# Second feed-forward block: transposing three of four groups by 32x32 blocks on VectorE and sixteen SBUF transfers instead of on TensorE

## The chip, the cores and the metric

One core of a Trainium2 chip runs the whole program. The metric is the device time of one execution in microseconds (us).

## The reference, cut to what matters

Two transformer-like blocks of width 2048 run one after the other over 256 rows. Each has a feed-forward part with 8192 inner columns; all weights are float32.

```python
# first block
m = rms_norm(h, pre_mlp_norm[i]) @ w_up[i]
m = jnp.square(jax.nn.relu(m)) @ w_down[i]
# second block
def sq_relu_mlp(h, w1, w2):
    return jnp.square(jax.nn.relu(h @ w1)) @ w2
```

The hidden rows `square(relu(x @ w1))` come out of the first product with tokens on the 128 partitions. The second product needs them with the inner columns on the partitions, so every hidden 128x128 square has to be transposed.

## The kernel before, in words

Every product of the kernel is cut into **chunks** of 512 output columns, and a chunk into **pieces** of 256 rows of weight (eight pieces for a depth of 2048). SyncE loads a piece (512 KB) into one of four slots of `raw`; ScalarE copies it rounded into `whi` (L706); VectorE subtracts, `wlo = raw - whi` (L1936); TensorE then makes twelve matmuls of 128x128 by 128x512: high by high, low by high, high by low (L1400). The loops run the same pieces in the same order on every engine and are tied by counting semaphores: SyncE loads piece p when VectorE has done piece p-4, ScalarE splits piece p+3 when TensorE has done piece p-1. A function `chunk(..., extra={u: f})` on an engine calls `f` just before it handles its u-th piece of that chunk; on ScalarE and VectorE that is the split of the piece three further on, on SyncE `f` comes after the load.

The feed-forward part `mlp` runs four blocks (`i`, NSB = 4) of 2048 inner columns. A block is eight chunks (`SEQ`): U0 to U3 make the hidden columns, D0 to D3 multiply them by the second weight matrix. After chunk U*c*:

- ScalarE evacuates PSUM with Relu into `rrow` (L903), GpSimd squares it into `sqrow` (L2681), each in two instructions of 128x512.
- In the next chunk TensorE makes eight 128x128 transposes of `sqrow` into two PSUM banks, ahead of its piece 3 (`turn_hidden`, L1610).
- At slot 4 of that chunk (`TURN_U`) ScalarE copies the two banks to `hhi` (L894) and VectorE makes `hlo` from them (L2208).

Those four inner groups of 512 columns feed D0 to D3. In the last block of the first feed-forward part and in the second block of the second one, SyncE also loads `w_mod` (L647) and VectorE multiplies it (L2142), at some of the slots. In chunk 17 of the second part, slot 6, ScalarE's queue writes a column of 2048 single numbers to DRAM (`gate_column_out`, L957).

Of the kernel before, what the change touches and what calls it, by code (L numbers as in the profile page):

```python
# [7 lines left out]
ALU = mybir.AluOpType  # L8
# [6 lines left out]
P = 128  # L15
# [5 lines left out]
HD = 128  # L21
# [102 lines left out]
def build(nc, I, out):  # L124

    ctx = ExitStack()
    with ctx:
# [143 lines left out]

        scratch = nc.dram_tensor("x_mid", (P, TH, D), F32, kind="Internal").ap()
# [36 lines left out]
        early_in = sem("early_in")  # L309
# [16 lines left out]
        gqk_in = sem("gqk_in")  # L326
# [25 lines left out]
        e_out = sem("e_out")  # L352
        e_in = sem("e_in")
        lb_out = sem("lb_out")
        lb_rows = sem("lb_rows")
# [201 lines left out]

        block = ctx.enter_context(nc.Block())
# [3 lines left out]
        def _(sp):  # L562
# [26 lines left out]
            def head_gains():  # L589
                for n, name in enumerate(("q_norm", "k_norm")):  # L590
                    sp.dma_start(g2[:, n], bass.AP(I[name].tensor, 0, [[0, P], [1, HD]])).then_inc(gqk_in, 16)

            def tables():
                sp.dma_start(early[:], I["k_early"]).then_inc(early_in, 16)
# [103 lines left out]
        def _(act):  # L698
# [75 lines left out]
            def spread_gains():  # L774
                act.wait_ge(gqk_in, 32)
# [108 lines left out]
            def mlp(k, u0, scale, extras):  # L884
                p0, g0 = plan[k]
                t0 = TG[k][0]
                for i in range(NSB):
                    for j, (kind, c) in enumerate(SEQ):
                        g = g0 + len(SEQ) * i + j

                        def turned(c=SEQ[j - 1][1], i=i):
                            for h in range(2):
                                act.wait_ge(t_done, i * 8 + (t0 + 2 * c + h + 1))
# [4 lines left out]
                        def relu(c=c, i=i, g=g):  # L898
                            act.wait_ge(sq_done, i * 8 + (2 * (u0 + c) + 2))
                            if scale and i == 0 and c == 0:  # L900
                                act.wait_ge(rstd_done, RMS["norm1"] + 1)
                            for th in range(TH):
# [5 lines left out]
                              extra=merge(extras.get(len(SEQ) * i + j, {}), {TURN_U: turned} if j and SEQ[j - 1][0] == "U" else {}))  # L908

            def embedding_out():  # L910
                act.wait_ge(acc_free, plan["mlp1"][1] + 2)
                act.dma_start(e_scratch, erow[:]).then_inc(e_out, 16)

            def context_in():
                act.wait_ge(e_out, 16)
# [49 lines left out]
            def embedding_in():  # L965
                act.wait_ge(t_done, TG["normc"][0] + 8)
                act.dma_start(erow[:], e_scratch).then_inc(e_in, 16)
# [145 lines left out]
            for c in range(14):  # L1113
# [7 lines left out]
                elif c < 12:  # L1121
                    if c == 10:
                        act.wait_ge(spill, 16)
# [190 lines left out]
            def row_squares(th):  # L1314
                act.wait_ge(reload, 16)
# [57 lines left out]
        def _(pe):  # L1373
# [224 lines left out]
            def mlp(k, u0, extras, first):  # L1598
                p0, g0 = plan[k]
                t0 = TG[k][0]  # L1600
                for i in range(NSB):
                    for j, (kind, c) in enumerate(SEQ):
                        def turn_hidden(c=SEQ[j - 1][1], i=i):
                            pe.wait_ge(sq_done, i * 8 + (2 * (u0 + c) + 4))
                            for h in range(2):
# [6 lines left out]
                                ins.then_inc(t_done, 1)  # L1612

                        def hidden(u, i=i):
                            return (lambda: pe.wait_ge(t_hi, i * 8 + (TG[k][1] + u + 1))), (lambda: pe.wait_ge(t_free, i * 8 + (t0 + u + 1)))
# [1145 lines left out]
```

## Time and profile before

| | us |
|---|---|
| median of three runs (2822.43 to 2824.7) | 2822.73 |
| the profiled execution's own time | 2820.31 |
| its span | 2818.7 |
| TensorE busy in the span | 2782.9 |
| VectorE busy | 1997.9 |
| ScalarE busy | 1374.9 |
| GpSimd busy | 146.9 |

The span is the time between the first and the last instruction; the execution's own time has some 1.6 us around it. TensorE's busy time is a sum over overlapping matmuls, so it says that the engine is nearly always occupied and not that it is at its peak. The granted TensorE clock over the span is 0.996 of the full 2.4 GHz.

### The profile page before, as it was taken

What the parts mean: (1) busy time and instruction counts of PE and PEld (TensorE: products, weight loads), DVE (VectorE), ACT (ScalarE), POOL (GpSimd) and SP (SyncE); (2) the same over time, 40 slices, a digit from 0 to 9 for tenths busy, and PEclk for the clock granted to TensorE, in tenths of its full rate; (3) what the DMA queues carried; (4) which work ended last, traced back from release to release, by engine and by line L of the source; (5) the groups of instructions that cost most, each with busy time, mean ns of one, the idle gap of its engine ahead of it and who ended that gap; (6) DMA issues with size and microseconds to landing.
All of it is one profiled execution on the core that took longest, in us unless ns stands there. A gap on an engine that the chain in (4) does not pass through costs nothing.

```text
span 2818.7 us, 34529 instructions
## 1 busy us (share of the span) xinstructions
PE 2782.9 (99%) x12939; PEld 2314.6 (82%) x12939; DVE 1997.9 (71%) x2268; ACT 1374.9 (49%) x1719; POOL 146.9 (5%) x109
## 2 busy tenths in 40 slices
PE   9999999999999999999999999999989999999998
PEld 7887888888888888788888888898878888888887
DVE  5666877899997676757785488687975467754455
ACT  5446454443443455557444445754554444344443
POOL 0000010010000100000000001000001000010010
PEclk9999999999999999999999999999999999999999
DMA  8963887888888777555666666408855588775654
GB/s 256 215 203 108 279 277 267 280 273 284 287 277 309 260 252 234 196 194 171 217 192 198 198 182 186 134 6 309 307 183 182 193 276 275 255 202 190 191 186 157
DMA packets 332780, 623.09 MB, mean 221 GB/s; under 512 B 37015, under 2 KB 38807, under 8 KB 330903
## 3 DMA queue, kind: packets, MB, share of 16 engines
q1 hardware_dynamic: 323543, 601.52, 66.8%
q10 hardware_dynamic: 9088, 19.56, 1.9%
q8 instruction: 95, 1.56, 0.2%
q14 instruction: 54, 0.44, 0.0%
HBM read 614.68 MB, written 7.27 MB: 221 GB/s over the span
## 4 chain that ended last, share of the span: by engine, by line
PE 93%; DVE 3%; DMA 2%; ACT 1%; issue 1%; SPq 0%; DVEq 0%; POOLq 0%; POOL 0%; ACTq 0%
PE ps L1400 86%; DMA raw<-w_in 1%; PE ps L1379 1%; PE ps L1610 1%; PE ps L1813 1%; PE ps L1793 1%; DMA raw<-w_o 1%; PE ps L1421 1%; DVE wlo L1936 1%; PE ps L1831 1%; PE ps L1532 0%; ACT whi L706 0%; PE ps L1512 0%; DVE macc L2142 0%; DVE cf L2291 0%
## 5 line engine op out<-in xcount | busy, mean ns | idle before, releaser
L1936 DVE TENSOR_TENSOR wlo<-raw,whi 128x1024 fp32r<-128x1024 f32 x940 | 1168.5, 1249 | 731.3 <-ACT whi L706 726.8
L706 ACT ACTIVATE whi<-raw 128x1024 fp32r<-128x1024 f32 x939 | 994.9, 1060 | 1222.6 <-PE ps L1400 1111.2
L1400 PE MATMUL ps<-whi,hhi 128*128 128x512 f32 x2032 | 549.5, 392 | 1.5 <-DVE yrow L2159 1.5
L1400 PE MATMUL ps<-whi,hlo 128*128 128x512 f32 x2032 | 544.0, 389 | 0.0
L1400 PE MATMUL ps<-wlo,hhi 128*128 128x512 f32 x2032 | 543.4, 389 | 0.2 <-DVE wlo L1936 0.2
L1400 PEld LDWEIGHTS ps<-wlo,hhi 128*128 128x128 f32 x2032 | 381.4, 188 | 80.1 <-DVE wlo L1936 0.6
L1400 PEld LDWEIGHTS ps<-whi,hlo 128*128 128x128 f32 x2032 | 381.1, 188 | 79.7
L1400 PE MATMUL ps<-whi,xhi 128*128 128x512 f32 x1632 | 442.7, 393 | 1.6 <-issue 1.6
L1400 PEld LDWEIGHTS ps<-whi,hhi 128*128 128x128 f32 x2032 | 378.3, 188 | 79.5 <-DVE yrow L2159 1.9
L1400 PE MATMUL ps<-whi,xlo 128*128 128x512 f32 x1632 | 440.1, 392 | 0.0
L1400 PE MATMUL ps<-wlo,xhi 128*128 128x512 f32 x1632 | 437.8, 390 | 0.0
L2142 DVE SCALAR_TENSOR_TENSOR macc<-mraw,cols,macc 128x512 f32<-128x512 f32 x504 | 367.1, 758 | 4.5
L1400 PEld LDWEIGHTS ps<-wlo,xhi 128*128 128x128 f32 x1632 | 307.5, 188 | 64.5
L1400 PEld LDWEIGHTS ps<-whi,xlo 128*128 128x128 f32 x1632 | 306.1, 188 | 63.5
L1400 PEld LDWEIGHTS ps<-whi,xhi 128*128 128x128 f32 x1632 | 304.4, 189 | 62.8 <-issue 1.9
L2681 POOL TENSOR_TENSOR sqrow<-rrow 128x512 f32<-128x512 f32 x64 | 93.1, 1475 | 1154.3 <-ACT rrow L903 1154.3
L2390 DVE SCALAR_TENSOR_TENSOR yT<-uT,cols,yT 128x252 f32<-128x252 f32 (+17 forms) x144 | 52.8, 428 | 0.0
L2661 POOL TENSOR_TENSOR stat<-stat 128x2 f32<-128x2 f32 x9 | 9.8, 1085 | 643.0 <-DVE stat L2148 442.4
L2208 DVE TENSOR_TENSOR hlo<-ps,hhi 128x512 fp32r<-128x512 f32 x64 | 41.0, 681 | 0.0
L1217 ACT ACTIVATE dec<-ps 128x1024 f32<-128x1024 f32 x32 | 32.5, 1023 | 17.1 <-PE ps L1793 10.5
L1813 PE MATMUL ps<-qD,kD 128*128 128x128 f32 x256 | 34.7, 279 | 3.6 <-DVE qD L2466 2.1
L1813 PEld LDWEIGHTS ps<-qD,kD 128*128 128x128 f32 x256 | 31.0, 191 | 5.1 <-DVE qD L2466 3.1
(312 smaller groups left out, 1476.6 us busy)
## 6 DMA issues: line engine op xcount, KB each, us to landing
raw<-w_in SPq DMA_DIRECT2D x296, 512.0 KB, 4.4
raw<-mlp_w SPq DMA_DIRECT2D x256, 512.0 KB, 3.8
mraw<-w_mod SPq DMA_DIRECT2D x384, 256.0 KB, 5.0
raw<-w_up SPq DMA_DIRECT2D x128, 512.0 KB, 4.6
raw<-w_down SPq DMA_DIRECT2D x128, 512.0 KB, 4.9
raw<-w_o SPq DMA_DIRECT2D x32, 512.0 KB, 5.3
raw<-w_ple_gate SPq DMA_DIRECT2D x32, 512.0 KB, 3.7
raw<-w_out SPq DMA_DIRECT2D x32, 512.0 KB, 5.9
```

The lines of the kernel that those rows point to most:

```text
L706: nc.scalar.activation(whi[:, s % NSLOT], raw[:, s % NSLOT], ACT.Copy).then_inc(hi_done, 1)
L1217: nc.scalar.activation(dst, src, ACT.Exp).then_inc(d_done, 1)
L1379: ins = nc.tensor.transpose(ps[:, TB[t % 2], c:c + P], src, ident)
L1400: ins = nc.tensor.matmul(ps[:, bank(par) + th], a[:, kt, th * P:(th + 1) * P], b[:, (s + u) % NSLOT, k], start=(kt == 0 and m == 0), stop= ...
L1421: ins = nc.tensor.matmul(ps[:, bank(g) + th], a[:, kt, th * P:(th + 1) * P], b[:, u % NSLOT, k], start=kt == 0 and m == 0, stop=kt == KT - ...
L1610: ins = nc.tensor.transpose(ps[:, TB[(t0 + h) % 2], a * T + th * P:a * T + (th + 1) * P], sqrow[:, th, f:f + P], ident)
L1813: ins = nc.tensor.matmul(o[:, (2 * hh + n) * P:(2 * hh + n + 1) * P], k[:, hh, n * P:(n + 1) * P], q[:, hh, t * P:(t + 1) * P], start=True ...
L1936: nc.vector.tensor_tensor(wlo[:, s % NSLOT], raw[:, s % NSLOT], whi[:, s % NSLOT].bitcast(F32), ALU.subtract)\
L2142: ins = nc.vector.scalar_tensor_tensor(out=a, in0=w, scalar=x, in1=a, op0=ALU.mult, op1=ALU.add)
L2208: nc.vector.tensor_tensor(hlo[:, kt:kt + 2], ps[:, TB[(t0 + h) % 2]].rearrange("p (a b) -> p a b", a=2), hhi[:, kt:kt + 2].bitcast(F32), A ...
L2390: nc.vector.scalar_tensor_tensor(out=y, in0=tap_part(uT[:, ct], ct, dd, True), scalar=wcol(TAPS // 2 + dd, ct), in1=y, op0=ALU.mult, op1=A ...
L2681: nc.gpsimd.tensor_tensor(sqrow[:, th], rrow[:, th], rrow[:, th], ALU.mult).then_inc(sq_done, 1)
```

## The change

For groups 0 to 2 of every block of the second feed-forward part, and of the last block of the first part, TensorE no longer transposes: 15 of the 32 groups. In their place, in the chunk after U*c*: at slot 2 VectorE makes two transposes of 32x32 blocks, `sqrow` to `hturned`; SyncE moves the blocks to their partitions by sixteen transfers of 32 partitions by 1 KB from `hturned` to `hgather`, queued behind its load of piece 1 of the chunk after next; at slot 7 ScalarE copies `hgather` to `hhi` and VectorE subtracts to `hlo`. `hturned` lies where `rrow` lies and `hgather` where `sqrow` lies, so the next Relu waits for the sixteen transfers and the next squares for `hlo`. Group 3 stays on TensorE. GpSimd's two loops over the blocks are written out, and some semaphores are merged (the head gains and the tables; the spills and the reloads).

```diff
+        BLK = P // STACK
+        hturned = at("hturned", [P, STACK, TH, STACK, BLK], F32, work_at + 32 * K)
+        hgather = at("hgather", [P, STACK, TH, STACK, BLK], F32, work_at + 36 * K)
...
+        def by_blocks(k, i, c):
+            return c < 3 and (k == "mlp2" or i == NSB - 1)
...
+            def blocks_moved(k, i, c):
+                n = VIA.index((k, i, c))
+                sp.wait_ge(ht_done, n + 1)
+                for g in range(STACK):
+                    for b in range(STACK):
+                        sp.dma_start(hgather[BLK * g:BLK * (g + 1), b], hturned[BLK * b:BLK * (b + 1), g]).then_inc(ht_in, 16)
...
+                        if 2 <= j <= 4 and by_blocks(k, i, j - 2):
+                            extra = merge(extra, {1: lambda i=i, j=j: blocks_moved(k, i, j - 2)})
...
             def spread_gains():
-                act.wait_ge(gqk_in, 32)
+                act.wait_ge(tables_in, 48)
...
+                        def blocks_high(c=j - 1, i=i):
+                            n = VIA.index((k, i, c))
+                            act.wait_ge(ht_in, 16 * STACK * STACK * (n + 1))
+                            for th in range(TH):
+                                nc.scalar.activation(hhi[:, 4 * c:4 * c + 4, th * P:(th + 1) * P].rearrange("p k (i b) -> p k i b", b=BLK),
+                                                     hgather[:, :, th].rearrange("p i k b -> p k i b"), ACT.Copy).then_inc(t_hi, 1)
...
                         def relu(c=c, i=i, g=g):
...
+                            if 1 <= c and by_blocks(k, i, c - 1):
+                                act.wait_ge(ht_in, 16 * STACK * STACK * (VIA.index((k, i, c - 1)) + 1))
...
-                              inserts=merge(extras.get(n, {}), {3: turn_hidden} if j and SEQ[j - 1][0] == "U" else {}, sum_inserts(k, n)),
+                              inserts=merge(extras.get(n, {}), {3: turn_hidden} if 1 <= j <= 4 and not by_blocks(k, i, j - 1) else {}, sum_inserts(k, n)),
...
+                        def blocks_turned(c=j - 1, i=i):
+                            dve.wait_ge(sq_done, i * 8 + 2 * (u0 + c) + 4)
+                            for th in range(TH):
+                                ins = nc.vector.transpose(hturned[:, :, th], sqrow[:, th].rearrange("p (k g b) -> p g k b", k=STACK, g=STACK))
+                            ins.then_inc(ht_done, 1)
+
+                        def blocks_low(c=j - 1, i=i):
+                            for th in range(TH):
+                                dve.wait_ge(t_hi, i * 8 + (h0 + 2 * c + th + 1))
+                                cs = slice(th * P, (th + 1) * P)
+                                nc.vector.tensor_tensor(hlo[:, 4 * c:4 * c + 4, cs].rearrange("p k (i b) -> p k i b", b=BLK),
+                                                        hgather[:, :, th].rearrange("p i k b -> p k i b"),
+                                                        hhi[:, 4 * c:4 * c + 4, cs].rearrange("p k (i b) -> p k i b", b=BLK).bitcast(F32),
+                                                        ALU.subtract).then_inc(t_free, 1)
...
+                                          {} if j < 1 or j > 4 else {2: blocks_turned, 7: blocks_low} if by_blocks(k, i, j - 1) else {TURN_U: turned}))
...
-                            pool.wait_ge(t_done, i * 8 + (TG[k][0] + 2 * c))
+                            if c and by_blocks(k, i, c - 1):
+                                pool.wait_ge(t_free, TG[k][0] + 8 * i + 2 * c)
```

## Rows read from the trace of the kernel before

**Rows 1.** The page: span, busy time by engine, chain of waits by engine.
```profile
span 2818.7 us, 34529 instructions
...
PE 2782.9 (99%) x12939; PEld 2314.6 (82%) x12939; DVE 1997.9 (71%) x2268; ACT 1374.9 (49%) x1719; POOL 146.9 (5%) x109
...
PE 93%; DVE 3%; DMA 2%; ACT 1%; issue 1%; SPq 0%; DVEq 0%; POOLq 0%; POOL 0%; ACTq 0%
```

**Rows 2.** Waits of TensorE, 2080 to 2800 us: total, times, longest.
```profile
PE ps L1379 <- ACT xs L1342: 6.5, 1, 6.5
PE ps L1400 <- issue: 1.6, 1, 1.6
```

**Rows 3.** Timeline of TensorE in chunk 17: start, duration, line, operation, [idle before].
```profile
2476.46 1.07 PE L1400 MATMUL ps<-whi,xhi 128*128 128x512 f32 x4
...
2479.18 1.07 PE L1400 MATMUL ps<-whi,xhi 128*128 128x512 f32 x4
...
2484.62 1.04 PE L1610 MATMUL ps<-small,sqrow 128*128 128x128 f32 x8
...
2499.12 1.07 PE L1400 MATMUL ps<-whi,xhi 128*128 128x512 f32 x4
```

**Rows 4.** Timeline of GpSimd, the squares of chunk 16.
```profile
2477.90 3.02 POOL L2681 TENSOR_TENSOR sqrow<-rrow 128x512 f32<-128x512 f32 x2 [107.15 <-ACT rrow L903]
```

**Rows 5.** Timeline of VectorE in chunk 17: splits of its pieces 4 and 5.
```profile
2480.88 1.21 DVE L1936 TENSOR_TENSOR wlo<-raw,whi 128x1024 fp32r<-128x1024 f32 x1
2483.25 1.23 DVE L1936 TENSOR_TENSOR wlo<-raw,whi 128x1024 fp32r<-128x1024 f32 x1 [1.16 <-ACT whi L706]
```

**Rows 6.** Timeline of VectorE in the block with w_mod: the products at slot 2.
```profile
2303.75 1.53 DVE L2142 SCALAR_TENSOR_TENSOR macc<-mraw,cols,macc 128x512 f32<-128x512 f32 x2
```

**Rows 7.** VectorE's groups by shape, whole span: busy us, mean ns | idle before.
```profile
L2208 DVE TENSOR_TENSOR hlo<-ps,hhi 128x512 fp32r<-128x512 f32 x64 | 41.0, 681 | 0.0
...
L2291 DVE RECIPROCAL rows<-rows 128x512 f32<-128x512 f32 x4 | 13.4, 3346 | 0.0
...
L2139 DVE TENSOR_SCALAR macc<-mraw,cols 128x512 f32<-128x512 f32 x8 | 3.7, 479 | 0.0
```

**Rows 8.** SyncE's issues by line: ns min/median/max, first and last start in us.
```profile
L600 SPq DMA_DIRECT2D raw<-mlp_w x256: 367/368/1099, 2068.9 to 2791.0; - x128
...
L617 SPq DMA_DIRECT2D bm<-bias_rows x32: 573/616/3060, 84.8 to 129.2; - x32
```

**Rows 9.** Timeline of SyncE near the start: small loads issued one behind another.
```profile
12.21 0.42 SPq L583 DMA_DIRECT2D vecs<-pre_ple_norm  x1
12.67 0.42 SPq L583 DMA_DIRECT2D vecs<-norm_pre_mix  x1
```

**Rows 10.** Landing time of the weight loads (L600) issued from 2440 to 2480 us.
```profile
DMA to landing us min/median/max: 3.5/4.0/4.6
```

**Rows 11.** DMA issues by line: size and median us to landing.
```profile
out<-res SPq DMA_DIRECT2D x8, 256.0 KB, 2.5
...
row_columns<-mcol ACTq DMA_DIRECT2D x1, 8.0 KB, 13.3
```

**Rows 12.** Timeline of ScalarE in chunks 17 and 18.
```profile
2476.66 1.09 ACT L903 ACTIVATE rrow<-ps 128x512 f32<-128x512 f32 x2 [1.60 <-PE ps L1400]
...
2479.43 1.06 ACT L706 ACTIVATE whi<-raw 128x1024 fp32r<-128x1024 f32 x1 [0.75 <-PE ps L1400]
...
2491.25 0.38 ACTq L957 DMA_DIRECT2D row_columns<-mcol  x1
...
2506.98 1.06 ACT L706 ACTIVATE whi<-raw 128x1024 fp32r<-128x1024 f32 x1 [5.63 <-DMA raw<-mlp_w]
```

**Rows 13.** A stretch of 5 us: busy of each engine, TensorE clock, DMA share, GB/s.
```profile
2496.00:2501.00 5.00, 5.00 (x24) 4.14 (x23) 1.49 (x2) 2.74 (x4) 0.43 (x1) 1.00 0.87 37
```

**Rows 14.** Lines of the merged semaphore: the tables' load, the copy that waits.
```profile
L594 SPq DMA_DIRECT2D early<-k_early x1: 468/468/468, 62.0 to 62.0; - x1
...
L777 ACT ACTIVATE gqk<-g x2: 398/720/1043, 82.0 to 83.0; 128x1024 f32<-128x1024 f32 x1, 128x256 f32<-128x256 f32 x1
```

More of the change, by code:

```diff
@@ L556, in build, with skipped, hidden_turned @@
             tc = [tc[0] + groups, tc[1] + groups * counted]
+        def by_blocks(k, i, c):
+            return c < 3 and (k == "mlp2" or i == NSB - 1)
+        VIA = [(k, i, c) for k in ("mlp1", "mlp2") for i in range(NSB) for c in range(4) if by_blocks(k, i, c)]
+        def skipped(k, i, c):
+            return 2 * sum(by_blocks(k, i, b) for b in range(c))
+        def hidden_turned(k, i, c, h):
+            return TG[k][0] + 8 * i + 2 * c + h + 1 - (skipped(k, i, c) if c < 3 else 0)
         block = ctx.enter_context(nc.Block())
@@ L907, in mlp @@
                         chunk(p0 + 8 * (len(SEQ) * i + j), evac,
-                              extra=merge(extras.get(len(SEQ) * i + j, {}), {TURN_U: turned} if j and SEQ[j - 1][0] == "U" else {}))
+                              extra=merge(extras.get(len(SEQ) * i + j, {}), {} if j < 1 or j > 4 else
+                                          {7: blocks_high} if by_blocks(k, i, j - 1) else {TURN_U: turned}))
             def embedding_out():
                 act.wait_ge(acc_free, plan["mlp1"][1] + 2)
-                act.dma_start(e_scratch, erow[:]).then_inc(e_out, 16)
+                act.dma_start(e_scratch, erow[:]).then_inc(spill, 16)
             def context_in():
-                act.wait_ge(e_out, 16)
+                act.wait_ge(spill, 16)
                 act.dma_start(trow[:], rows_of(I["ctx_2"][0])).then_inc(ctx_in, 16)
@@ L2217, in mlp @@
                               extra=merge(extras.get(n, {}), mod_totals(k, n), mod_extra(k, n, mod_product),
-                                          {TURN_U: turned} if j and SEQ[j - 1][0] == "U" else {}))
+                                          {} if j < 1 or j > 4 else {2: blocks_turned, 7: blocks_low} if by_blocks(k, i, j - 1) else {TURN_U: turned}))
             NM, NP, NX = 5 * KT, 4 * KT, 2 * KT
@@ L2273, in _ @@
             d_first = c_first + 32
-            mlp("mlp1", place({0: lambda: post0_res(3), 1: low1(3), 2: low1(4), 3: low1(5), 4: low1(6), 5: low1(7), 6: norm1_mean_square,
+            mlp("mlp1", 0, place({0: lambda: post0_res(3), 1: low1(3), 2: low1(4), 3: low1(5), 4: low1(6), 5: low1(7), 6: norm1_mean_square,
                                c_first + 5: mod_of_mixer, c_first + 6: mixer_gains,
@@ L2618, in _ @@
             last = 8 * (len(SEQ) * NSB - 4)
-            mlp("mlp2", place({0: lambda: [low4(0), norm4_row(2)], 1: lambda: [low4(1), norm4_row(3)],
+            mlp("mlp2", 16, place({0: lambda: [low4(0), norm4_row(2)], 1: lambda: [low4(1), norm4_row(3)],
                                **{g: (lambda g=g: low4(g)) for g in range(2, 8)}, 137: last_mods, **{last + 8 * c + 13: (lambda c=c: post4_gain(c)) for c in range(3)}}))
@@ L2678, in mlp @@
                             pool.wait_ge(acc_free, i * len(SEQ) + (g0 + j + 2))
-                            pool.wait_ge(t_done, i * 8 + (TG[k][0] + 2 * c))
+                            if c and by_blocks(k, i, c - 1):
+                                pool.wait_ge(t_free, TG[k][0] + 8 * i + 2 * c)
+                            elif c:
+                                pool.wait_ge(t_done, hidden_turned(k, i, c - 1, 1))
+                            else:
+                                pool.wait_ge(t_done, TG[k][0] + 8 * i)
                             nc.gpsimd.tensor_tensor(sqrow[:, th], rrow[:, th], rrow[:, th], ALU.mult).then_inc(sq_done, 1)
-            with pool.Fori(0, NSB) as i:
+            for i in range(NSB):
                 mlp(i, "mlp1")
@@ L2731, in _ @@
             nc.gpsimd.tensor_tensor(stat[:, 10:12], stat[:, 4:6], stat[:, 64:66], ALU.pow).then_inc(rstd_done, 1)
-            with pool.Fori(0, NSB) as i:
+            for i in range(NSB):
                 mlp(i, "mlp2")
```

34 lines of the change are left out of this document (17 added, 17 removed).

## The prediction, made before the changed kernel ran

> **What bounds the kernel now.** I read the page first: TensorE is busy 99% of the span and holds 93% of the chain that ended last [rows 1]. The waits of TensorE over the second feed-forward part come next: two waits, 8.1 us in all, at its very beginning [rows 2]; from there to the end it waits for nobody. So time falls here only by taking work from TensorE, and rises only if something is late enough to make it wait. The third view is its timeline in chunk 17, the one that transposes group 0 of block 2 [rows 3]. A piece of twelve matmuls takes 2479.18 - 2476.46 = 2.72 us. Between pieces 2 and 3 stand eight transposes, and the whole chunk lasts 2499.12 - 2476.46 = 22.66 us, against 8 x 2.72 = 21.76 us without them: a group costs 0.90 us of the bound engine.
>
> **TensorE's part.** 15 groups go: 15 x 0.90 = 13.5 us, all on the path. Group 3 of each block stays, as do the 17 groups outside the condition.
>
> **VectorE's part.** Two block transposes of 128x512 come in at slot 2. The trace has no such instruction; its 128x512 operations lie between 0.48 us and 3.35 us, and most of them at 0.68 us [rows 7]. I take 0.68 us, as the subtraction that it stands beside, and keep 1.0 to 6.7 us for the two. In chunk 17 the squares end at 2477.90 + 3.02 = 2480.9 [rows 4], and VectorE is free from 2480.88 + 1.21 = 2482.1 [rows 5]: it doesn't wait for them. The two end at 2483.5, the split of piece 5 behind them at 2484.7 instead of 2484.5. At the upper end that split would end at 2490.0; TensorE needs it 1.8 us (two thirds of a piece) into piece 5, at 2476.46 + 13.6 + 1.8 = 2491.9, so even that is covered by the three pieces that the splits are ahead. Where w_mod is multiplied (6 of the 15 groups) 1.53 us of products stand ahead at slot 2 [rows 6] and the split comes about 1.4 us later than before. `hlo` costs two instructions of the same size as before [rows 7]; the copies to `hhi` likewise. They only move from slot 4 to slot 7, and TensorE wants group 2, the last of them, four pieces later in D0.
>
> **SyncE's part.** This is where the change can lose. Sixteen issues stand in the in-order queue between the loads of piece 1 and piece 2 of the chunk after next. Load 1 follows the split of piece 5, which VectorE does after its transposes, so SyncE's new wait adds nothing. No issue between SBUF addresses is in the trace. Bounds: 0.37 us, a weight load [rows 8], and 3.06 us, the longest bias load, among 32 whose median is 0.62 us [rows 8]. I take 0.46 us, the step from one small load to the next [rows 9], as the nearest in size: 16 x 0.46 = 7.4 us. In chunk 17: load 1 at 2484.7, transfers from 2485.1 to 2492.5, then load 2, some 5 us later than now; it lands 4.0 us later [rows 10], at 2496.5, and its split by ScalarE (1.06 us) ends at 2497.6. TensorE comes to that piece ten pieces after the chunk's start, at 2476.46 + 27.2 = 2503.7. Cover left: 6.1 us. With 0.62 us it is 3.6 us; the cover is gone at 0.46 + 6.1 / 16 = 0.84 us a transfer, and the gain of the group at 0.90 us. In the groups with w_mod, 1.4 us later, 4.7 us are left (at 0.62 us 2.1 us). Both upper bounds together, 0.62 us and 6.7 us of transposes, make these six groups 3.2 us late each and the other nine 1.7 us.
>
> That a late load alone does no harm is seen in the trace: at 2506.98 ScalarE had waited 5.63 us for a load [rows 12], and TensorE had no wait there [rows 2].
>
> **The transfers' landing.** The last is issued at 2492.0; the fastest kind in the trace lands in 2.5 us, the slowest in 13.3 [rows 11]. I take 2.5, the plain transfer: 2494.5. ScalarE comes to slot 7 six pieces and one split in, 2476.46 + 16.3 + 1.3 = 2494.1, waits 0.4 us, copies for 1.2 us and is ready for load 2 at 2495.7, before that has landed. Behind the wait stand that split, the next Relu (2498.2, unmoved) and with it the next squares. To make TensorE late the landing must come after 2503.7 - 1.06 - 1.2 = 2501.4, that is take 9.4 us.
>
> The Trainium skill speaks against this part: "DMA: Bandwidth & Descriptors", section "Anatomy of one DMA", puts a fixed cost of about 2.0 us on every transfer, and its "Rules for kernel authors" say that below 64 KB one pays mostly overhead and should join small transfers. These are 32 KB each. The same section says that most of the fixed cost is the wait for the last byte's receipt, and small loads issued 0.46 us apart [rows 9] agree that the queue doesn't hold the next issue for it; what it does if the transfers follow one another is rival 4, priced from rows there.
>
> **One place without cover.** In chunk 17, slot 6, ScalarE's queue starts the column write; it lands 13.3 us later [rows 11], and meanwhile the DMA engines move 37 GB/s at 87% busy [rows 13]. Now the loads of pieces 2 and 3 of chunk 18 have landed by then, or almost; with the change they are issued after 2492.5, into it. The write starts 0.9 us earlier, at about 2490.4, and holds until 2503.7. I estimate load 2 at 2504.5, split at 2505.6, against 2503.7: TensorE waits 2 us, once (0 to 4). It also stands behind about five of the transfers, which keeps the 4.
>
> **Edits at nothing.** The merged semaphores: the copy of head gains now also waits for the tables, whose load starts at 62.0, 20 us before that copy [rows 14]; the spills and reloads keep their order. GpSimd's loops written out: it is busy 5% of the span [rows 1]. If any of these covers failed, TensorE would wait at one place, once.
>
> **The sum.** 2820.31 (the profiled execution: 2818.7 of span and 1.6 around it) - 13.5 + 2.0 = 2808.8. The runs' median is 2.4 us above that execution, so on the median 2822.73 - 11.5 = 2811.2.
>
> **Rivals.**
> 1. Full cover, the column write included: 2822.73 - 13.5 = 2809.2. For it: the 5.63 us wait without effect [rows 12]. Against: no loads were held back then.
> 2. Partial cover. The six groups with w_mod, or the ones after a slow issue, lose 1 to 2 us each. Six at 1.5 us give 2811.2 + 9 = 2820; with the least loss, 0.5 us, 2814. It takes issues above 0.62 us or transposes near 3.35 us. For it: the bias loads' 0.62 us [rows 8]; against: these have more and shorter rows.
> 3. Slower: SyncE's queue becomes the bound. From 0.90 us a transfer each group loses more than it gains. At 1.2 us the sixteen take 19.2 us, 11.8 us more than my sum; less 6.1 us of cover (4.7 in six groups) TensorE waits 5.7 us nine times and 7.1 us six times, 94 us: 2811.2 + 94 = 2905. For it: single bias loads up to 3.06 us [rows 8]. Against: their median, and weight loads at 0.37 us.
> 4. Slower too, by another mechanism: the transfers don't overlap. Each 2.5 us behind the other [rows 11], the last lands 40 us after 2485.1, at 2525; ScalarE, stopped at slot 7, has the split ready at 2527.4, 23.7 us late, 15 times: 2811.2 + 356 = 3167. It decides from (2501.4 - 2485.1) / 16 = 1.0 us a transfer. It is the rule on small transfers taken at its word.
> 5. The change doesn't do what it says: TensorE is not the bound in these chunks and the time stays at 2822.7. Rows 2 and 3 speak against it; nothing for it.
>
> **How the numbers follow.** Chances: forecast 0.60, full cover 0.17, partial 0.11, SyncE's queue 0.07, transfers in a row 0.04, no effect 0.01. The range reaches from 2807.5, 1.7 us below full cover for the spread of a median (the three runs spread 2.3 us), to 2820, the dear end of partial cover; past it lie rivals 3 to 5 and the rest of 2, some 0.14. A difference under 0.2% (5.6 us, so above 2817.1) can't be told from none here. Forecast, full cover and half of partial are faster, 0.82; the other half and no effect are the same, 0.07; rivals 3 and 4 are slower, 0.11.
>
> **What would show it.** Right: chunks that lose the transposes last 21.76 us; no transposes but group 3's; sixteen issues in about 7.4 us, the next load some 5 us late; ScalarE's waits moved to the transfers and loads at slot 7 without a wait of TensorE, save one near the column write. Wrong: waits of TensorE for `whi` or `wlo` at piece 2 of a chunk (SyncE's queue), issues above 0.84 us, a landing above 9 us, or transposes so long that the splits fall behind.

## The result and the profile after

The changed kernel is slower. Its median is 2834.39 us (six runs, 2832.74 to 2836.83) against 2822.58 us of the kernel before on the same chip: a ratio of 1.0046, 95% interval 1.0036 to 1.0056, 11.8 us. Forecast were 2811.2 us in a range of 2807.5 to 2820. The profiled execution took 2835.27 us.

The page answers to [rows 1]: TensorE is busy 4.9 us less (forecast were 13.5; behind some waits its matmuls take longer, as shown further down), the span is 14.8 us longer, and ten points of the chain that ended last have gone from TensorE to VectorE, to SyncE's transfers (L674) and to DMA. In the first line of the last pair stand shares by engine, in the second by line.

```profile
span 2833.5 us, 34492 instructions
...
PE 2778.0 (98%) x12819; PEld 2304.9 (81%) x12819; DVE 2022.2 (71%) x2298; ACT 1377.7 (49%) x1719; POOL 143.8 (5%) x109
...
PE 83%; DVE 5%; SPq 4%; DMA 3%; issue 2%; ACT 2%; POOL 0%; DVEq 0%; POOLq 0%; ACTq 0%
PE ps L1434 76%; SPq L674 4%; DVE wlo L1971 2%; DMA raw<-mlp_w 1%; PE ps L1413 1%; PE ps L1848 1%; ACT whi L730 1%; PE ps L1828 1%; DVE macc L2177 1%; DMA raw<-w_o 1%; DMA hgather<-hturned 1%; PE ps L1455 1%; PE ps L1644 1%; PE ps L1866 1%; DVE hturned L2242 0%
```

The waits of TensorE in the second part after the change (in total, times, longest) answer to [rows 2]. The two old ones stand; 13.2 us are new, for ScalarE's split and for GpSimd's squares (ahead of group 3's transposes, L1644).

```profile
PE ps L1434 <- ACT whi L730: 10.0, 7, 3.1
PE ps L1413 <- ACT xs L1376: 6.6, 1, 6.6
PE ps L1644 <- POOL sqrow L2736: 3.2, 3, 1.1
PE ps L1434 <- issue: 1.6, 1, 1.6
```

The new instructions after the change (ns min/median/max; then the landing) answer to [rows 7, 8 and 11]: the block transposes are as forecast, 0.68 us; the landing too, 2.1 us for 2.5; an issue takes 0.59 us for 0.46, and 0.04 us lie between two.

```profile
L674 SPq DMA_DIRECT2D hgather<-hturned x240: 507/591/1482, 925.6 to 2735.2; - x120
...
L2242 DVE STREAM_TRANSPOSE hturned<-sqrow x30: 661/684/707, 922.7 to 2723.6; 128x512 f32<-128x512 f32 x30
...
  ACT hhi L919: 72.8, 15
...
DMA to landing us min/median/max: 1.8/2.1/10.5
```

The indented line is the point: ScalarE, which was to wait 0.4 us a group, waited 72.8 us in 15 groups. What comes before that wait is seen in the chain of waits after the change, here for the third group of block 0 (start, duration, what; of the sixteen transfers the first and the last are shown):

```profile
2169.02 4.07 DMA raw<-mlp_w
...
2173.11 0.04 ACT whi L730
...
2176.12 3.26 DVE wlo L1971 x2
2179.39 1.22 DVE hturned L2242 x2
2180.60 1.12 DVE wlo L1971
...
2181.74 0.37 SPq L615
...
2182.15 0.51 SPq L674
...
2191.83 0.59 SPq L674
...
2192.47 1.84 DMA hgather<-hturned
```

What follows is in the timeline of ScalarE after the change (start, duration; in brackets the idle time before and what ended it):

```profile
2194.33 1.16 ACT L919 ACTIVATE hhi<-hgather 128x512 fp32r<-128x512 f32 x2 [6.04 <-DMA hgather<-hturned]
2197.11 1.06 ACT L730 ACTIVATE whi<-raw 128x1024 fp32r<-128x1024 f32 x1 [1.62 <-DMA raw<-mlp_w]
2198.08 1.07 ACT L936 ACTIVATE rrow<-ps 128x512 f32<-128x512 f32 x2
```

From the block transposes to the copy to `hhi` it is 14.9 us. But the copy is not the last wait: ScalarE then stands 1.62 us more for a weight load, the one that SyncE issues behind the sixteen transfers, and only then come the split, the Relu and the squares. So it is in 12 of the 15 groups, by 1.5 to 2.0 us; in the other three this load lands just as the copies end. The timeline of GpSimd after the change shows the squares of one chunk and of the next.

```profile
2175.22 3.09 POOL L2736 TENSOR_TENSOR sqrow<-rrow 128x512 f32<-128x512 f32 x2 [20.10 <-ACT rrow L936]
2199.22 3.09 POOL L2736 TENSOR_TENSOR sqrow<-rrow 128x512 f32<-128x512 f32 x2 [20.91 <-ACT rrow L936]
```

They are 24.00 us apart, where a chunk without transposes lasts 21.76 us. The split behind the late load is as far from the one before it (2197.11 - 2173.11 = 24.00), and the chain says why. In its first lines the load behind the sixteen transfers of the group before lands (at 2173.09); its split, the Relu and the next split follow on ScalarE, then VectorE's splits (until 2179.38), behind them the block transposes, then the load of piece 1, the sixteen issues, and the next load behind them. That is a closed round, longer than a chunk; each group of a block starts later than the one before it, against TensorE. A second round runs beside it, over the landing of the sixteen and ScalarE's stop at slot 7. Without the 1.62 us for the load the 24.00 would be some 22.4 us (an estimate): that round too is longer than a chunk, but the shorter of the two.

To find where the time went, I subtracted the start of the n-th split of VectorE in the trace of before from that in each other trace (940 splits in both). Change of that difference by stage, in us, negative where time is won; three whole groups are worth 2.7 us. One profile scatters by some 2 us in stages where nothing is changed (third column).

```
kernel                   first part,  stage   unchanged  second part, block
                         last block   behind  stages     0     1 (w_mod)  2 (column)  3
after                      +1.1       +4.8     0.0      -0.9     +5.8       +4.7     -1.2
e1 one transfer            -2.7       +2.9    +1.6      -2.7     -2.7       -2.7     -2.7
e2 four batches            +8.1       +4.5    +2.5      +2.3    +16.6      +13.0     +3.3
e3 without w_mod            0.0       +0.2    +0.4      -1.5      0.0       +4.9     -1.1
e4 GpSimd's queue          -2.0       +3.1    +1.8      -2.7     +4.8       +4.2     -2.7
e5 through DRAM            -2.7       +2.4    +1.6      -2.7     +0.2       +3.9     -2.7
e9 queue alone             +1.8       -1.3    -0.7       0.0     +3.7       +3.2      0.0
e10 one late               +2.1       +3.0    -0.3      -2.7     +7.0       +5.2     -2.7
e11 loop open               0.0       +0.2    +2.0      +1.4    +10.0       +7.5     +1.7
e12 loop open, GpSimd       0.0       -0.7    +2.3      -2.7     -2.7       -2.7     -2.7
e13 loop open, half         0.0       -1.6    +0.1      -2.7     -2.7       -2.7     -2.7
e14 half each              -2.7       +4.1    +0.1      -2.7     -2.7       -2.7     -2.7
```

So most of the loss of the changed kernel lies in the two blocks with `w_mod`, in the block with the column write, and in the stage behind the first part; the two plain blocks (0 and 3) win 0.9 and 1.2 us where each should win 2.7.

### The profile page after: what moved, and what is told of

It is laid out like the page before. It is cut to its first block, busy times and chain, and to the rows that moved or that the text cites. A ratio compares the mean times of both kernels' runs of the same rounds, so it can differ in the third digit from the quotient of the medians.

```text
span 2833.5 us, 34492 instructions
## 1 busy us (share of the span) xinstructions
PE 2778.0 (98%) x12819; PEld 2304.9 (81%) x12819; DVE 2022.2 (71%) x2298; ACT 1377.7 (49%) x1719; POOL 143.8 (5%) x109
## 4 chain that ended last, share of the span: by engine, by line
PE 83%; DVE 5%; SPq 4%; DMA 3%; issue 2%; ACT 2%; POOL 0%; DVEq 0%; POOLq 0%; ACTq 0%
PE ps L1434 76%; SPq L674 4%; DVE wlo L1971 2%; DMA raw<-mlp_w 1%; PE ps L1413 1%; PE ps L1848 1%; ACT whi L730 1%; PE ps L1828 1%; DVE macc L2177 1%; DMA raw<-w_o 1%; DMA hgather<-hturned 1%; PE ps L1455 1%; PE ps L1644 1%; PE ps L1866 1%; DVE hturned L2242 0%
## 5 line engine op out<-in xcount | busy, mean ns | idle before, releaser
L2177 DVE SCALAR_TENSOR_TENSOR macc<-mraw,cols,macc 128x512 f32<-128x512 f32 x504 | 373.7, 773 | 4.6
L2249 DVE TENSOR_TENSOR hlo<-hgather,hhi 128x512 fp32r<-128x512 f32 x30 | 19.4, 689 | 63.9 <-ACT hhi L919 63.9
L919 ACT ACTIVATE hhi<-hgather 128x512 fp32r<-128x512 f32 x30 | 17.3, 626 | 72.8 <-DMA hgather<-hturned 72.8
L1251 ACT ACTIVATE dec<-ps 128x1024 f32<-128x1024 f32 x32 | 32.6, 1025 | 17.1 <-PE ps L1828 10.5
```

What stands on the lines that cost most here:

```text
L1251: nc.scalar.activation(dst, src, ACT.Exp).then_inc(d_done, 1)
L2177: ins = nc.vector.scalar_tensor_tensor(out=a, in0=w, scalar=x, in1=a, op0=ALU.mult, op1=ALU.add)
```

## The experiments

The kernel before had medians of 2819.53 us (beside e0 to e3), 2819.51 (e4, e5, e9, e10), 2819.86 (e11, e12) and 2821.16 (e13, e14); a difference is always against the one run beside it.

**e0, the edits alone.** No group goes by blocks; what is left are the merged semaphores and the written-out loops.

```diff
-            return c < 3 and (k == "mlp2" or i == NSB - 1)
+            return False
```

> All groups are transposed on TensorE again; only the written-out GpSimd loops and the merged semaphores of the change stay. Theory 1 (the loss is SyncE's sixteen issues, 0.63 us each in the changed kernel's trace, 10.1 us a group in front of the next weight loads): 2822.6, within 3 us. Rival (the other edits cost something: the changed kernel stands 1.3 us back after its first pieces and loses another 4.4 us near 1143 us, where no group is touched): about 2828.

Measured: 2819.64 us, ratio 1.0000 (0.9991 to 1.0009). The edits cost nothing.

**e1, one transfer.** One plain transfer of all 512 KB at the same place; the blocks are not moved to their partitions, so the hidden values are others.

```diff
-                for g in range(STACK):
-                    for b in range(STACK):
-                        sp.dma_start(hgather[BLK * g:BLK * (g + 1), b], hturned[BLK * b:BLK * (b + 1), g]).then_inc(ht_in, 16)
+                sp.dma_start(hgather[:], hturned[:]).then_inc(ht_in, 16)
```

> The sixteen transfers are one transfer of all 128 partitions and the same 512 KB, so the blocks don't reach their partitions and the hidden values of 15 groups are wrong. Theory 1 (issue time on SyncE): the waits of TensorE in the feed-forward parts vanish, 2834.4 less some 22 us, 2810 to 2816. Rival (the bytes between SBUF addresses take the DMA engines from the weights): no change, about 2834. Rival (the wait for the landing in front of ScalarE's splits): one transfer lands some 7 us earlier, so this too gives about 2812; the next run tells these two apart.

Measured: 2809.41 us, ratio 0.9964 (0.9950 to 0.9977), 10.1 us less. The timeline of ScalarE in e1 at the place of the chain above:

```profile
2182.65 1.14 ACT L917 ACTIVATE hhi<-hgather 128x512 fp32r<-128x512 f32 x2
...
2187.07 1.09 ACT L934 ACTIVATE rrow<-ps 128x512 f32<-128x512 f32 x2 [1.60 <-PE ps L1432]
```

And that of GpSimd in e1:

```profile
2166.47 3.02 POOL L2734 TENSOR_TENSOR sqrow<-rrow 128x512 f32<-128x512 f32 x2 [18.74 <-ACT rrow L934]
2188.23 3.02 POOL L2734 TENSOR_TENSOR sqrow<-rrow 128x512 f32<-128x512 f32 x2 [18.74 <-ACT rrow L934]
```

ScalarE doesn't stop, the Relu waits for TensorE as it should, and the squares are 21.76 us apart. Every block gains its 2.7 us, also the one with the column write. Neither the bytes nor VectorE's work nor the longer way through `hgather` costs anything: the sixteen issues do, or what waits for them.

**e2, four batches of four transfers**, behind the loads of pieces 1 to 4, so that no load waits for more than four issues.

```diff
-                            extra = merge(extra, {1: lambda i=i, j=j: blocks_moved(k, i, j - 2)})
+                            extra = merge(extra, {1 + g: lambda i=i, j=j, g=g: blocks_moved(k, i, j - 2, g) for g in range(STACK)})
```

> The sixteen transfers are issued four at a time, behind the loads of pieces 1, 2, 3 and 4. Theory 1: no load is held back by more than 2.5 us, so TensorE doesn't wait in groups without the column write; 2811 to 2816. Rival (ScalarE stops at slot 7 for the landing and is late with its splits): the last transfer is issued some 2 to 3 us later than in one burst, so more waits, 2836 to 2850.

Measured: 2865.98 us, ratio 1.0160 (1.0146 to 1.0174). That is slower than either expectation. Spreading the issues didn't help: the last transfer lands later still, and ScalarE stops for longer. ScalarE's wait in e2, from 2080 us to the end:

```profile
ACT hhi L918 <- DMA hgather<-hturned: 106.7, 12, 13.4
```

**e3, without the blocks that have w_mod**: nine groups.

```diff
-            return c < 3 and (k == "mlp2" or i == NSB - 1)
+            return c < 3 and k == "mlp2" and i != 1
```

> Only the nine groups of the second part's blocks 0, 2 and 3 by blocks; the six groups beside w_mod loads are transposed on TensorE. By the trace of the changed kernel the six lose 12.3 us and gain 5.4, the nine lose 10.4 and gain 8.1. Theory 1 (SyncE's queue has less room where it loads w_mod too): 2834.4 less 7, about 2827.5, and less than that if the 5.8 us outside the groups goes as well. Rival (each group costs the same 0.8 us net wherever it stands): 2822.6 + 9 x 0.8 = 2830.

Measured: 2824.27 us, ratio 1.0013 (1.0004 to 1.0023), 4.7 us more than before. Without the blocks with `w_mod` and without groups ahead of the stage behind the first part more than half of the loss is gone, but the column write's block still loses 4.9 us, and the plain ones win 1.1 to 1.5 instead of 2.7.

**e4, the same sixteen on GpSimd's queue.** No weight load stands behind them.

```diff
-                        sp.dma_start(hgather[BLK * g:BLK * (g + 1), b], hturned[BLK * b:BLK * (b + 1), g]).then_inc(ht_in, 16)
...
+                                    pool.dma_start(hgather[BLK * g:BLK * (g + 1), b], hturned[BLK * b:BLK * (b + 1), g]).then_inc(ht_in, 16)
```

> The same sixteen transfers, issued from GpSimd's queue behind the squares, not from SyncE's. Theory 1 as it stands after the first runs (a closed loop: VectorE's transposes, 10.1 us of issues, the landing, ScalarE stopped at slot 7, the next Relu, squares, the next transposes; it takes 23.2 to 26 us a round in the changed kernel against 21.76 us of a chunk): it depends on GpSimd's issue time, which no trace here shows; at 0.5 us or less the sixteen land before ScalarE comes to slot 7 and the time is 2808 to 2811; at 1 us or more the loop is longer than on SyncE, 2840 or above, though no weight load is held back. Rival (the loss is the weight loads held back in SyncE's queue): 2808 to 2812 at any issue time.

Measured: 2828.15 us, ratio 1.0036 (1.0023 to 1.0050). The issues in e4 (ns; who waited; landing):

```profile
L2732 POOL DMA_DIRECT2D hgather<-hturned x240: 496/496/697, 922.5 to 2720.4; - x120
...
  ACT hhi L910: 65.8, 15
...
DMA to landing us min/median/max: 2.4/4.7/13.5
```

Both expectations missed: the issues take 0.50 us, but the transfers land in 4.7 us (median) instead of 2.1. With no load held back ScalarE stops for nearly as long, and the blocks with `w_mod` and the column write lose nearly as much. The plain ones gain in full; so what they lose in the changed kernel goes with the held-back load.

**e5, through DRAM**: one transfer out and four back, five issues.

```diff
+                sp.dma_start(h_blocks, hturned[:].rearrange("p g t k b -> p g (t k b)")).then_inc(ht_out, 16)
...
+                    sp.dma_start(hgather[BLK * g:BLK * (g + 1)].rearrange("p i t k b -> p i (t k b)"), src).then_inc(ht_in, 16)
```

> The gather goes through a DRAM buffer: one transfer of 512 KB out behind load 1, four transfers of 128 KB back behind load 2; five issues, some 3 us of SyncE. Loop theory: out lands some 4 us after its issue, the last of the four back some 5 us later, at about the time that ScalarE comes to slot 7: waits of 0 to 2 us there, 2809 to 2816. Rival (held-back loads): load 3 waits 2 to 4 us at most, 2810. Rival (bytes on the DMA engines): another 15 MB of DRAM traffic in 15 groups, and slower than the changed kernel, 2834 or more.

Measured: 2820.70 us, ratio 1.0005 (0.9996 to 1.0014). The plain blocks gain in full, the one with `w_mod` loses what it gains, the one with the column write more. There are five issues instead of sixteen, but two landings in a row, and the time is above the 2809 to 2816 expected.

**e9, the queue alone.** TensorE transposes all groups as before; SyncE issues sixteen transfers of the same shape at the 15 places, from a table to an unused buffer, and no engine waits for them in the groups.

```diff
-                        sp.dma_start(hgather[BLK * g:BLK * (g + 1), b], hturned[BLK * b:BLK * (b + 1), g]).then_inc(ht_in, 16)
+                        sp.dma_start(spare[BLK * g:BLK * (g + 1), b], small[BLK * b:BLK * (b + 1)]).then_inc(ht_in, 16)
```

> TensorE transposes all groups as in the kernel before; SyncE also issues sixteen transfers of the same shape at the 15 places, from a constant table to a spare buffer, and nothing waits for them but the next sixteen. Loop theory: the held-back loads alone cost TensorE nothing in the nine groups without w_mod and up to 2 us in each of the six with it; 2819.5 to 2826. Rival (held-back loads are the loss): the changed kernel's loss without its gain, 2819.5 + 12 + 13.5 = 2845.

Measured: 2828.52 us, ratio 1.0033 (1.0021 to 1.0045): 9.0 us, between the two expectations. The queue costs something by itself: nothing in plain blocks, 3.7 and 3.2 us where `w_mod` or the column write comes on top, by loads that land late. A round has more room here than in the changed kernel, for a chunk with transposes lasts 22.66 us. ScalarE's wait in e9, from 2080 us to the end:

```profile
ACT whi L735 <- DMA raw<-mlp_w: 91.3, 39, 10.1
```

**e10, one late transfer**: e1's single transfer, issued behind the load of piece 4.

```diff
-                            extra = merge(extra, {1: lambda i=i, j=j: blocks_moved(k, i, j - 2)})
+                            extra = merge(extra, {4: lambda i=i, j=j: blocks_moved(k, i, j - 2)})
```

> One transfer of all 128 partitions, as in the run with one transfer (the hidden values of 15 groups are wrong), but issued behind load 4 and not load 1. SyncE is busy with it for 0.4 us. It lands about as late after the transposes as the sixteen, some 15 us. Loop theory: ScalarE waits 3 us at slot 7 and the rounds take some 24 us; 2825 to 2840. Rival (held-back loads): as with one early transfer, 2809.4.

Measured: 2831.55 us, ratio 1.0047 (1.0034 to 1.0061). The issue in e10, who waited, the landing:

```profile
L672 SPq DMA_DIRECT2D hgather<-hturned x15: 478/510/634, 931.6 to 2727.1; - x15
...
  ACT hhi L917: 95.6, 15
...
DMA to landing us min/median/max: 5.3/6.7/12.6
```

One issue of half a microsecond, put late, loses as much as sixteen put early; put early (e1) it loses nothing. So a late last landing is enough by itself, without a load held back; here too the plain blocks gain in full and the loss is in the others.

**e11, the round opened** (the 12 groups of the second part). `hturned` and `hgather` get room of their own, no Relu waits for the transfers, and `hhi` and `hlo` are made at slot 0 of the chunk after next; the sixteen stay on SyncE.

```diff
-                            if 1 <= c and by_blocks(k, i, c - 1):
-                                act.wait_ge(ht_in, 16 * STACK * STACK * (VIA.index((k, i, c - 1)) + 1))
...
-                                          {7: blocks_high} if by_blocks(k, i, j - 1) else {TURN_U: turned}))
+                              extra=merge(extras.get(len(SEQ) * i + j, {}), {0: blocks_high} if 2 <= j <= 4 and by_blocks(k, i, j - 2) else {},
```

> Block groups in the second part alone (12 groups, worth 12 x 0.9 = 10.9 us of TensorE). hturned and hgather get room of their own, so that no Relu waits for a transfer, and ScalarE and VectorE take the gathered values at slot 0 of the chunk after next, some 6 us later than slot 7. The sixteen transfers stay on SyncE. Theory (a loop from the block transposes over sixteen issues and the last landing to ScalarE's stop at slot 7, its next Relu, the squares and the next transposes is longer than a chunk): the loop is cut, the chunks last 21.76 us, TensorE waits for ScalarE's split at most in the groups with w_mod and at the column write, where weight loads are held back; time 2819.5 - 10.9 = 2808.6 plus 0 to 7 us of held loads: 2809 to 2816. Rival (the sixteen issues in SyncE's queue are the whole loss, by the weight loads behind them): cutting the loop changes nothing, the loss by group stays as in the changed kernel, 2826 or more.

Measured: 2840.98 us, ratio 1.0071 (1.0058 to 1.0085). My theory missed by 25 us, and the rival's 2826 or more came true: with the stop at slot 7 gone, the loss is larger. From 2080 us on ScalarE has no wait for `hgather` left, but one for weights, and the chain of waits of e11 shows the round through the weight loads alone. First the wait:

```profile
ACT whi L731 <- DMA raw<-mlp_w: 164.0, 58, 10.8
```

The chain (start, duration, what; the sixteen transfers left out):

```profile
2153.04 1.22 DVE hturned L2243 x2
2154.25 1.12 DVE wlo L1970
...
2155.39 0.37 SPq L615
...
2165.92 3.94 DMA raw<-mlp_w
...
2172.47 2.45 DVE hlo L2250 x2
...
2175.02 2.35 DVE wlo L1970 x2
2177.36 1.21 DVE hturned L2243 x2
```

The sixteen take SyncE to 2165.9; the next load lands at 2169.9; ScalarE and VectorE do their work on it, with `hlo` now among it; the next block transposes stand behind: 2177.36 - 2153.04 = 24.3 us. The sixteen are the longest stretch in this round. In the changed kernel the same round takes 23.2 to 24.0 us in the blocks without `w_mod`.

**e12, the same with the transfers on GpSimd's queue.**

```diff
-                        sp.dma_start(hgather[BLK * g:BLK * (g + 1), b], hturned[BLK * b:BLK * (b + 1), g]).then_inc(ht_in, 16)
...
+                            pool.wait_ge(t_free, TG[k][0] + 8 * i + 2 * c)
...
+                                    pool.dma_start(hgather[BLK * g:BLK * (g + 1), b], hturned[BLK * b:BLK * (b + 1), g]).then_inc(ht_in, 16)
```

> The same with the sixteen transfers issued on GpSimd's queue, so that no weight load stands behind them. Theory (loop and held loads, each with its part): both are gone; 2808.6 to 2811, no wait of TensorE in the second part but the two at its start. Rival (the loop alone is the loss, the queue costs nothing): the same time as with the transfers on SyncE, within 1 us. Third (sixteen small transfers load the DMA engines and delay the weights whoever issues them): waits of TensorE for the split stay, 2815 or more.

Measured: 2809.66 us, ratio 0.9963 (0.9949 to 0.9977), 10.2 us less than before where 12 x 0.9 = 10.8 were to be had, within the 2808.6 to 2811 expected. TensorE's waits from 2080 us on in e12 are the two of [rows 2] and no other:

```profile
PE ps L1402 <- ACT xs L1365: 6.5, 1, 6.5
PE ps L1423 <- issue: 1.6, 1, 1.6
```

**e14, eight transfers on each queue**: the changed kernel with its 15 groups, its slot 7 and its shared buffers.

```diff
-                for g in range(STACK):
+                for g in range(2):
...
+                            for g in range(2, STACK):
+                                for b in range(STACK):
+                                    pool.dma_start(hgather[BLK * g:BLK * (g + 1), b], hturned[BLK * b:BLK * (b + 1), g]).then_inc(ht_in2, 16)
```

> The changed kernel with all its 15 groups and its slot 7, but eight of the sixteen transfers on SyncE's queue and eight on GpSimd's. Theory (two loops longer than a chunk, one through the last landing and ScalarE's slot 7, one through the weight loads behind the sixteen issues): eight issues take 5.1 us instead of 10.1, the last landing comes 10.3 us after the block transposes start instead of 14.7, before ScalarE gets to slot 7 (12.2 us with one transfer), and the next loads are held 5 us instead of 10. Both loops are then shorter than 21.76 us and nothing adds up: the full 13.5 us, less about 3 given back at the first part's end and 0 to 3 at the column write: 2809 to 2813. Rival (each issue costs in proportion, wherever the sum stands): half of the 25 us that the changed kernel loses on its full gain comes back, 2821 to 2823.

Measured: 2813.94 us, ratio 0.9972 (0.9962 to 0.9981), 7.2 us less than before. (The expectation's 2809 to 2813 was worked out from a kernel before of 2819.5; this one had 2821.16.) ScalarE's waits for the transfers from 2080 to 2800 us are 8.3 us in e14 (below) instead of 60.0 in the changed kernel, and TensorE waits nowhere but at the two places of [rows 2]; each block of the second part gains its 2.7 us.

```profile
ACT hhi L921 <- DMA hgather<-hturned: 8.3, 3, 6.2
```

**e13, the opened round with eight on each queue** (12 groups; the same split of the transfers in e11).

> The opened loop (12 groups, gathered values taken at slot 0 of the chunk after next), eight transfers on SyncE and eight on GpSimd. Theory: the loop through the weight loads, 24.3 us with sixteen issues on SyncE (block transposes, issues, landing of the next load, copies and splits), falls by 5.1 us to 19.2, under a chunk's 21.76: no waits of TensorE for the split, 2808.6 to 2811. Rival (in proportion): half of the 31 us between the two versions of the opened loop, about 2825.

Measured: 2812.98 us, ratio 0.9970 (0.9958 to 0.9981), 8.2 us less than before; that is above the 2808.6 to 2811 expected, which again started from 2819.5. Its profile gains 2.7 us in every block. Halving the issues on SyncE took away not half of e11's loss but all of it. The loss is that of a round against a chunk, with a threshold, not a price for each issue.

## Why the prediction was wrong, by its own steps

**TensorE's part** held: a group is worth 0.9 us wherever nothing holds TensorE up (e1, e12 to e14: 2.7 us for three groups). One thing was overlooked. The statement that TensorE waits for nobody was read from the second part alone [rows 2]; behind the first part's last block there is a stage with a wait of its own. Here are the waits of TensorE from 880 to 1200 us after the change.

```profile
PE ps L1413 <- DVE hlo L1989: 4.6, 1, 4.6
PE ps L1434 <- ACT whi L730: 2.4, 2, 1.7
PE ps L1644 <- POOL sqrow L2736: 1.2, 1, 1.2
```

The first is 2.3 us long in the kernel before. In e1, which gains 2.7 us ahead of it, TensorE comes earlier and waits 4.6 us there, so that the gain of these three groups is given back; in e14 too. In the changed kernel, which comes to the stage with a loss, the wait is 4.6 us as well, so an earlier TensorE is not its whole cause. The kernels with no block groups ahead of this stage (e3, e11, e12, e13) lose nothing there (0.2 us at the most). 12 x 0.9, not 15, were to be had.

**VectorE's part and the edits at nothing** held: 0.684 us a transpose, e0 at ratio 1.0000. (That most of VectorE's 128x512 operations take 0.68 us was misread: the most frequent, the product with `w_mod`, takes 0.76 us. Nothing hung on it.)

**SyncE's part** was mis-sized: 16 x 0.635 us (0.59 and the gap of 0.04) = 10.2 us and not 7.4. By the prediction's own account that was no harm: at 0.62 us it left 3.6 us of cover (3.5 by its numbers), 2.1 with `w_mod`. But this cover was worked out for one group that finds all splits three pieces ahead. A held-back load that lands late leaves the next group with less, and the account doesn't carry that over. e9, where only the queue is left, loses 0.0 in the plain blocks and 3.7 with `w_mod`.

**The transfers' landing is the step that failed**, at the words "the next Relu (2498.2, unmoved) and with it the next squares". The prediction held its two late comers, the last transfer and the load behind the sixteen, against the moment when TensorE needs the split (2503.7, 6.1 us of cover). But the Relu stands behind that split in ScalarE's queue, and for it the prediction's own numbers leave 0.6 us: the load lands at 2496.5, its split ends at 2497.6, the Relu is due at 2498.2. The 2.8 us that the issues took longer are enough to move it.

Measured, ScalarE waited twice in a group. For the transfers it was 2.42 us in the first group of block 0 (forecast 0.4; the longer issues, less 0.4 us of quicker landing, make 2.8), then 3.72 and 6.04 us. After the copies it waited 1.57, 1.71 and 1.62 us more for the load, so that the load, and not the landing, set the Relu. Splits, squares and block transposes are behind the Relu, issues behind the transposes: the delay comes round. From one group of a block to the next, the landings of that load are 23.2 to 24.0 us apart in blocks 0, 2 and 3 of the second part and 24.5 to 26.5 us in the two blocks with `w_mod`. I priced the wait once for each group and asked whether TensorE would feel it ("take 9.4 us"); I should have added up the round and compared it with 21.76 us.

Both rounds go through the sixteen issues, and either one alone costs time: the one over the landing in e10 (one issue, late: slower by 12.0 us) and e4 (no load behind the sixteen: slower by 8.6 us), in both without a loss in the plain blocks; the queue and its held-back loads in e9 (slower by 9.0 us) and e11 (21.1 us). With both short (e1, e12, e13, e14) the second part's gain is there in full. So it is shown that the loss comes from rounds through the sixteen issues that are longer than a chunk; how the loss in the blocks with `w_mod` and the column write divides between the two rounds is not separated.

**With w_mod** the products at slot 2 lengthen either round; the forecast's rival 2 (partial cover) had the place and the condition, an issue above 0.62 us (0.635 with the gap), but 1.5 us for each group where block 1 lost 5.8 + 2.7 = 8.5 us, 2.8 a group.

**The column write** was priced by the weight loads that it delays, 2 us; e9 measures 3.2 us for that. Not foreseen was that seven of the sixteen small transfers, those issued after the write began at 2501.79 us, fall into it as well. The timeline of ScalarE in the changed kernel there:

```profile
2515.14 1.15 ACT L919 ACTIVATE hhi<-hgather 128x512 fp32r<-128x512 f32 x2 [9.60 <-DMA hgather<-hturned]
2517.27 1.07 ACT L936 ACTIVATE rrow<-ps 128x512 f32<-128x512 f32 x2
```

The longest landing is 10.5 us, above the 9.4 us that the prediction named as its limit; the block gained nothing and lost 4.7 us.

**TensorE's clock** added to it. After the wait of 3.15 us that ends at 2381 us and that of 2.15 us that ends at 2517 us the mean granted clock of the next 9 us is 0.81 in the changed kernel; before the waits it was 1.00. The clock is 1.2 GHz for part of the stretch, and 9 x (1 - 0.81) = 1.7 us of full speed are lost each time, which the sum of the waits doesn't hold. Against its full gain of 10.8 us the second part lost 19.2 us (10.8 and the 8.4 by which its four blocks are longer); 13.2 us are new waits, 3.4 us these two stretches, and the rest was not traced. The first two lines are from the timeline of TensorE (four matmuls take 1.07 us elsewhere), the others are sums over a stretch. Columns: span, busy time and count of PE, PEld, DVE, ACT and POOL, granted clock, DMA share, GB/s.

```profile
2381.49 2.04 PE L1434 MATMUL ps<-whi,hhi 128*128 128x512 f32 x4 [3.15 <-ACT whi L730]
2517.42 1.65 PE L1434 MATMUL ps<-whi,xhi 128*128 128x512 f32 x4 [2.15 <-ACT whi L730]
...
2372.00:2381.00 9.00, 6.34 (x28) 4.90 (x27) 2.52 (x3) 2.23 (x4) 0.00 (x0) 1.00 0.51 140
2381.00:2390.00 9.00, 8.51 (x35) 7.01 (x36) 8.49 (x8) 4.88 (x7) 2.55 (x2) 0.81 1.02 378
...
2518.00:2527.00 9.00, 9.00 (x34) 7.30 (x33) 7.55 (x8) 5.65 (x6) 2.10 (x2) 0.81 0.80 264
```

**The rivals.** SyncE's queue as the bound (2905 us) was refuted by its own price, 0.635 us against 0.90, and still the load held behind the queue was what the round waited for last. Transfers in a row (3167 us) didn't happen: they land 2.1 us after their issue, sixteen of them within 12 us. The Trainium skill, "DMA: Bandwidth & Descriptors", "Rules for kernel authors", wants small transfers joined. In e1 that wins, for another reason than the landing: its one transfer of 512 KB lands in 6.3 us (its median), where the chain of the changed kernel has 12.2 us from the first issue to the last landing (2194.31 - 2182.15), most of it issues. It is not the only way: e12 has the full gain in the second part with sixteen small ones. The fixed cost of about 2.0 us, which the prediction put on every transfer, stands in the section "Anatomy of one DMA" of that page of the Trainium skill for transfers issued from GpSimd. The landings from SyncE come near it, 1.8 us at the least and 2.1 us in the median; those from GpSimd in e4 are longer, 2.4 and 4.7 us.

**What stays open.** Why the stage behind the first part gives the gain back even when TensorE comes to it earlier: in e1 ScalarE does three splits of `w_in` there 2 to 3 us earlier than in the kernel before, but the fourth, behind a load, at 1119.42 us against 1117.81. A column of single numbers is written in that stage too; whether it delays the load was not tried. In e3 the plain blocks lose 1.2 to 1.6 us of their 2.7; in eight of its nine groups the held-back load again came last, but no run took it alone out of e3.

## What to carry to other kernels

When work goes from the bound engine to a way over several queues, write down every round that closes from one iteration to the next (who waits for whom, until the same instruction comes again), add up its steps, and compare the sum with the time of one iteration of the bound engine: below it the whole gain is there, above it the excess is paid each time, and cover worked out for one iteration says nothing. Hold each late comer against the first thing that stands behind it in its queue (here the Relu), not only against the bound engine. A wait put into an in-order queue delays all that stands behind it, so look at what those instructions release. Where a round is too long, shorten its longest stretch (here: half of the issues on another queue) before restructuring.

## What the runs showed of the hardware

- An issue of a transfer of 32 partitions x 1 KB between SBUF addresses holds SyncE's queue for 0.59 us, longer than that of a weight load of 512 KB (0.37 us, [rows 8]); GpSimd's queue issues the same in 0.50 us, SyncE one of 512 KB between SBUF addresses in 0.51 us (e1).
- The same transfer lands in 2.1 us (median) in the changed kernel, where SyncE issues no load between the sixteen, and in 4.7 us when GpSimd issues it and SyncE's loads run beside it (e4). The queue alone is not shown to be the reason: in e14, with eight on each queue, it is 4.1 us from SyncE and 4.2 us from GpSimd.
- While a column of 2048 single numbers is written to DRAM (12.3 us to landing in the changed kernel), transfers between SBUF addresses are slow as well: 9.24 us for the last of the sixteen in the chain of the changed kernel, against 1.84 us in block 0.
- A wait of TensorE of 2.15 us was followed by a granted clock of 0.81 over 9 us.
